# Rearranging the opening of a one-core encoder layer: two feature tiles first, and weight rests on GpSimd

## The reference

```python
x = _layernorm(x, ln_in_g, ln_in_b)
c_act = jax.nn.silu(c)
mod = (c_act @ w_ada[l] + b_ada[l]).reshape(B, N_SUBLAYERS, 3, D)
shift, scale, gate = mod[:, :, 0], mod[:, :, 1], mod[:, :, 2]

h = x * (1.0 + scale[:, 0, None, :]) + shift[:, 0, None, :]
y = _swiglu(h, ffn1_w_in[l], ffn1_w_out[l])
x = _layernorm(ALPHA * x + 0.5 * gate[:, 0, None, :] * y, post_ln_g[l, 0], post_ln_b[l, 0])
...
```

## Time and profile before

| | us |
|---|---|
| median of 3 timed runs | 955.99 (955.94 to 956.3) |
| the profiled execution: its time / its span | 956.35 / 954.6 |
| TensorE matmul busy | 938.6 (98% of the span) |
| VectorE busy | 506.7 (53%) |
| ScalarE busy | 375.0 (39%) |
| GpSimd busy | 267.3 (28%) |

### The profile page before, as it was taken

The page is one execution under the profiler, slowest core; times in us unless marked ns, Lnnn a source line. Parts: engine busy times, 40 slices in busy tenths (PEclk is TensorE's granted clock), DMA queues, the critical chain, the costliest instruction groups (busy, mean ns, idle before and its releaser), DMA issues.

```text
span 954.6 us, 10883 instructions
## 1 busy us (share of the span) xinstructions
PE 938.6 (98%) x4233; PEld 759.1 (80%) x4233; DVE 506.7 (53%) x713; ACT 375.0 (39%) x567; POOL 267.3 (28%) x222
## 2 busy tenths in 40 slices
PE   7999999999999999999999999999999999999997
PEld 5788888888888888788767687888888888888886
DVE  5956766545454865777666488632232222233334
ACT  6753223242222313564486556532322323221224
POOL 0021111111104512336843575611111111125125
PEclk9999999999999999999999999999999999999999
DMA  9836566556544663222521122232323222213302
GB/s 363 358 112 208 188 200 197 181 176 217 194 154 140 235 232 99 84 86 91 132 67 45 45 67 67 97 124 98 101 91 109 89 93 100 83 62 121 118 20 88
DMA packets 38499, 127.21 MB, mean 133 GB/s; under 512 B 4016, under 2 KB 6192, under 8 KB 38448
## 3 DMA queue, kind: packets, MB, share of 16 engines
q1 hardware_dynamic: 38448, 126.52, 39.4%
HBM read 123.36 MB, written 2.10 MB: 131 GB/s over the span
## 4 chain that ended last, share of the span: by engine, by line
PE 92%; DVE 3%; ACT 1%; POOL 1%; issue 1%; DMA 1%; SPq 0%; POOLq 0%; DVEq 0%; ACTq 0%
PE bank L601 28%; PE bank L603 28%; PE bank L602 28%; PE bank L957 1%; PE bank L981 1%; PE bank L680 1%; PE bank L686 1%; PE bank L687 1%; PE bank L968 1%; DMA x<-xT 1%; POOL cq L2014 0%; DVE w_lo L1081 0%; DVE lat L1534 0%; PE bank L727 0%; PE bank L874 0%
## 5 line engine op out<-in xcount | busy, mean ns | idle before, releaser
L1081 DVE TENSOR_TENSOR w_lo<-raw,w_hi 128x1024 fp32r<-128x1024 f32 x153 | 206.0, 1353 | 278.1 <-ACT w_hi L1053 277.7
L601 PE MATMUL bank<-h_hi,w_hi 128*128 128x512 f32 x727 | 284.5, 391 | 0.0
L603 PE MATMUL bank<-h_hi,w_lo 128*128 128x512 f32 x727 | 283.0, 389 | 0.0
L602 PE MATMUL bank<-h_lo,w_hi 128*128 128x512 f32 x727 | 282.9, 389 | 0.0
L1053 ACT ACTIVATE w_hi<-raw 128x1024 fp32r<-128x1024 f32 x153 | 155.9, 1031 | 189.2 <-PE bank L603 188.3
L1916 POOL TENSOR_TENSOR a_lo<-act_t,a_hi 128x512 fp32r<-128x512 f32 x44 | 58.9, 1339 | 422.0 <-ACT a_hi L1175 421.9
L601 PEld LDWEIGHTS bank<-h_hi,w_hi 128*128 128x128 f32 x727 | 136.6, 188 | 28.7 <-issue 0.5
L603 PEld LDWEIGHTS bank<-h_hi,w_lo 128*128 128x128 f32 x727 | 136.5, 188 | 28.5
L602 PEld LDWEIGHTS bank<-h_lo,w_hi 128*128 128x128 f32 x727 | 136.5, 188 | 27.8
L601 PE MATMUL bank<-a_hi,w_hi 128*128 128x512 f32 (+1 forms) x374 | 141.2, 377 | 0.0
L602 PE MATMUL bank<-a_lo,w_hi 128*128 128x512 f32 (+1 forms) x374 | 140.8, 377 | 0.0
(11 more groups left out here) (306 smaller groups left out, 1048.1 us busy)
## 6 DMA issues: line engine op xcount, KB each, us to landing
raw<-wunits SPq DMA_DIRECT2D x145, 512.0 KB, 3.2
ada_ring<-ada_w SPq DMA_DIRECT2D x56, 512.0 KB, 4.4
ada_first<-ada_w SPq DMA_DIRECT2D x16, 512.0 KB, 10.1
raw<-wunits SPq DMA_DIRECT2D x16, 384.0 KB, 2.9
x<-xT SPq DMA_DIRECT2D x4, 512.0 KB, 6.0
outT<-x SPq DMA_DIRECT2D x8, 256.0 KB, 2.6
K<-k_rope SPq DMA_DIRECT2D x2, 512.0 KB, 8.4
c_act<-c_rows SPq DMA_DIRECT2D x1, 512.0 KB, 7.9
```

The source lines that it names most:

```text
L601: mm(out, lh, rh, start=first, stop=False)
L602: mm(out, lh, rl, start=False, stop=False)
L603: return mm(out, ll, rh, start=False, stop=last)
L1081: nc.vector.tensor_tensor(lo, raw[:, slot, 0:width], hi.bitcast(F32), SUB).then_inc(s_lo, 1)
```

## The change

The x loads are eight instead of four, and unit 1 is loaded behind the first gate pair. ScalarE loads the table of Silu at the start, guesses the root ahead of rounding unit 0, normalises only the feature tiles 0 and 1 (256 columns of each token group) ahead of the first transposes, and rounds unit 1 ahead of h_hi[0] and unit 2 ahead of the affine tiles. GpSimd normalises tiles 2 and 3 and makes the rests of units 0 and 1. TensorE transposes tile 2 after tile 1's first matmuls. A few semaphores that nobody waited on go.

```diff
-X_LOADS = 4
+X_LOADS = 8
...
             unit(0)
+            ada_pair(0)
             unit(1)
-            ada_pair(0)
             ada_pair(1)
...
-                    if k + 2 < KD:
+                    if k == 1:
+                        pe.wait_ge(s_xnb, QB)
+                        transpose_x(2)
+                    if 1 <= k < KD - 2:
                         if k == 2:
                             pe.wait_ge(s_xna, 2 * QB)
                         transpose_x(k + 2)
...
+            preload(1, ACT.Silu)
             for t in range(QB):
                 act.wait_ge(s_bn, t + 1)
...
             preload(0, ACT.Abs_reciprocal_sqrt)
-            act_hi(act, 0)
             act.wait_ge(s_tv, 1)
             fn(trstd[:], tvar[:], ACT.Abs_reciprocal_sqrt).then_inc(s_tq, 1)
-            act_hi(act, 1)
-
-            def normal(t, i):
-                src = bank[TOKEN_BANK[i][t]][:] if i else x_tok[:, t, 0:TOK]
-                if i == 0:
-                    act.wait_ge(s_xk, t + 1)
-                fn(x_tok[:, t, i * TOK:(i + 1) * TOK], src, ACT.Identity,
+            act_hi(act, 0)
+
+            def normal_two(t):
+                act.wait_ge(s_xk, t + 1)
+                fn(x_tok[:, t, 0:2 * P], x_tok[:, t, 0:2 * P], ACT.Identity,
+                   scale=trstd[:, t:t + 1], bias=tshift[:, t:t + 1]).then_inc(s_xna, 1)
+
+            def normal_half(t):
+                fn(x_tok[:, t, TOK:2 * TOK], bank[TOKEN_BANK[1][t]][:], ACT.Identity,
                    scale=trstd[:, t:t + 1], bias=tshift[:, t:t + 1]).then_inc(s_xna, 1)
...
             for t in range(QB):
-                normal(t, 0)
+                normal_two(t)
+            act_hi(act, 1)
             act.wait_ge(s_tp, 1)
             act.wait_ge(s_full0, 2)
...
+            act_hi(act, 2)
             affine(0)
             affine(1)
-            act_hi(act, 2)
...
-                for n in range(2) if k == 0 else range(k + 1, min(k + 2, EARLY)):
+                if k == 1:
+                    dve.wait_ge(s_lo, 2)
+                for n in range(k + 1, min(k + 2, EARLY)) if k else ():
                     dve_lo(dve, n)
...
+            for n in range(2):
+                pool.wait_ge(s_hi, n + 1)
+                hi, lo = parts(n, 0, UNIT)
+                tt(lo, raw[:, n, :], hi.bitcast(F32), SUB).then_inc(s_lo, 1)
+            pool.wait_ge(s_tv, ROOT_STEPS)
+            for t in range(QB):
+                pool.wait_ge(s_xk, t + 1)
+                ts(x_tok[:, t, 2 * P:TOK], x_tok[:, t, 2 * P:TOK], trstd[:, t:t + 1], tshift[:, t:t + 1], MUL, ADD)\
+                    .then_inc(s_xnb, 1)
             ffn(0, 1, a_hi1, a_lo1)
```

More of the change, by code:

```diff
@@ L380, in build @@
         s_bn, s_tv = sem("x_stats"), sem("x_root")
-        s_xna = sem("x_normal")
+        s_xna, s_xnb = sem("x_normal"), sem("x_normal_by_pool")
         s_tok = sem("x_token_major")
@@ L394, in build @@
         s_nx = [None] + [sem(f"normal_steps{p}") for p in range(1, 4)]
-        s_hf = [sem(f"h_full{p}") for p in range(4)]
+        s_hf = [sem(f"h_full{p}") for p in range(3)]
         s_hh = [sem(f"h_hi_done{p}") for p in range(4)]
-        s_hl = [sem(f"h_lo_done{p}") for p in range(4)]
-        s_res = [sem(f"residual_scaled{p}") for p in range(4)]
+        s_hl = [sem(f"h_lo_done{p}") for p in range(3)]
+        s_res = [None] + [sem(f"residual_scaled{p}") for p in range(1, 3)]
         s_uh = [None] + [sem(f"plain_hi_done{p}") for p in range(1, 3)]
@@ L1275, in _ @@
                 if k < 3:
-                    normal(2 * k - 2, 1)
-                    normal(2 * k - 1, 1)
+                    normal_half(2 * k - 2)
+                    normal_half(2 * k - 1)
                 if k + 1 < KD:
```

## The result

| | before | after |
|---|---|---|
| median, compared on one chip | 956.07 us (7 runs) | 959.64 us (7 runs; 959.3 to 959.97) |
| the profiled execution: time / span | 956.35 / 954.6 | 959.3 / 957.5 |

The change makes the kernel slower by 0.36% (ratio 1.0036, 95% interval 1.0027 to 1.0045), 3.6 us between the medians and 2.9 us between the two profiled spans.

A forecast was written before the change was run, and what follows sets the result against it. TensorE is dense after the opening, so the start of tile 2's matmuls decides. The root gains 2.3 us, turns and moved transposes outweigh it, h_hi[2] comes 2.3 later: 955.99 + 2.3 = 958.3 us, range 955.0 to 959.6.

The forecast's parts named there:

- the main case: Opening: GpSimd's long subtractions hold VectorE in turns, and moved transposes delay tile 2; 958.3 us, span 957.1 to 959.2, chance 0.45.
- the third rival: Tiles 1 and 2: TensorE's clock stays low past 32 us, 1.2 us more, 959.5; chance 0.12.
- The root 2.3 us sooner: Opening: fewer transposes before the statistics, table load in idle time, guess ahead of rounding; root complete at 14.7, not 17.0.
- Two tiles first: ScalarE in the opening: four normals over 256 columns take 2.0 us, end 16.8; unit 1's rounding ends 17.8.
- VectorE and GpSimd take turns, tiny instructions too: Ahead of tile 0: VectorE's two-input instructions stand behind GpSimd's long subtractions; h_hi[0] starts at 22.0, 1.6 us later.
- Rival 1: Opening: GpSimd's work is hidden, full_col ready by 17.8; 954.1 to 955.3 us, likeliest 954.4; chance 0.16.
- rival 2: Opening: only wide VectorE instructions pay for turns; full_col ready at 19.5, h_hi[0] at 19.6; 957.6 us, chance 0.27.
- The multiply-adds: GpSimd's four 256-column normalisings: 0.53 us each alone; gate pair 1 still gives first_col[1] by 24.6 to 25.4.
- Transposes of tile 2 moved: Behind tile 1's four matmuls: affine(2) waits about 1 us extra, starts 29.6; h_hi[2] done at 32.8, +2.3.
- The sum: Whole kernel: h_hi[2]'s 2.3 us delay carried unshortened to the end; profiled run 958.65, median 958.3.
- Transfers change nothing: Loads of the opening: none added, later ones issued earlier behind a stream already full at 420 GB/s; no effect.

The follow-up runs named there:

- no_gpsimd: The changed kernel with GpSimd's rests and multiply-adds and the moved tile 2 transposes undone; early root, loads and ScalarE order stay: 954.5 us.
- rests_only: The kernel before, with only the rests of units 0 and 1 moved to GpSimd: 959.46 us.
- reading_beside: The kernel before plus four unused 512-column GpSimd additions on scratch from the root's end on: 961.26 us (one run).
- writing_beside: The kernel before plus ten 512-column GpSimd memsets, which only write scratch, from the root's end on: 956.0 us (one run).
- late_second_rest: The changed kernel, with GpSimd's second rest (unit 1) waiting for full_col: 960.42 us.
- transposes_only: The kernel before, with only tile 2's transposes moved behind tile 1's four matmuls: 957.44 us.
- scalar_normals_late: The changed kernel without its GpSimd work, ScalarE normalising all 512 columns; tile 2's transposes stay moved: 955.39 us.
- no_gpsimd_warm: The changed kernel without GpSimd work or moved transposes, with three instead of one extra matmuls ahead of tile 0's: 954.86 us.
- rests_on_vector: The changed kernel, with the rests of units 0 and 1 back on VectorE; GpSimd keeps the four multiply-adds: 956.6 us.
- kept_warm: The changed kernel with six instead of one idle matmuls between tile 0's transposes and h_hi[0]: 959.54 us.

## Why the prediction was right, and where its sizes were off

The forecast was 958.3 us, slower by 2.3; 959.64 was measured, slower by 3.6. That is at the upper edge of the whole range (959.6) and 0.4 above the 959.2 of the main case alone; the number lies nearer to the third rival's 959.5. That the main case is the right one is told by the trace, step by step, and not by the time.

- *The root 2.3 us sooner.* Right: 14.59 against 17.01 in the trace. The loads' share of it was 0.3 us and not 0.5 (the statistics end at 12.83 against 13.15). With the loads and the order on ScalarE, and without the rest of the change, it is worth 1.6 us of time (no_gpsimd).
- *Two tiles first.* 2.0 us for the four normals was 2.08. The narrowing bought nothing, since ScalarE then waited 4.4 us.
- *VectorE and GpSimd take turns, tiny instructions too.* Right, and close throughout: h_hi[0] at 21.98 (22.0), act_t[1] at 25.81 (25.8), h_hi[1] done at 27.29 (27.3). rests_only, reading_beside and writing_beside show the mechanism apart from the rest of the change. Rival 1 (GpSimd hides everything) and rival 2 (small ones slip in before a turn) fall with first_col's 2.17 us.
- *The multiply-adds.* The assumption "a multiply-add of 256 columns is 0.53" was wrong beside a busy VectorE: 7.85 us for four. The conclusion drawn from it, that they don't hold tile 1, held all the same (first_col[1] done at 24.52, predicted 24.6 to 25.4). That they might hold tile 2 the prediction never asked; in the changed kernel they tie with the matmuls, and in late_second_rest they do hold it.
- *Transposes of tile 2 moved.* The mis-sized step is "From 27.3 this gives 28.8 to 30.2; I take 29.6, with the clock recovering on the way at about 29 as before". affine(2) started at 30.37, just past the upper end. The four matmuls took 1.9 us, as taken; what was mis-sized is the time from the transposes' start to affine(2), for which 29.6 leaves 0.4 us and which measured 1.16 (29.21 to 30.37). About half of that excess goes with the clock, which did not recover (0.50 through the stretch at 30): in transposes_only, where it came back just as the transposes ran, the same piece took 0.76 (27.81 to 28.57). The other half was too short a term at either clock. That was rival 3's condition in a milder form: the clock was back at 31 and not past 32, tile 2's matmuls ran at full clock from 33.52 on, and only the transposes and the first matmul behind them were slow. This step's 0.8 us is more than all of what h_hi[2] missed (33.46 for 32.8). By itself the move was measured at +1.4 (transposes_only) and +0.9 (scalar_normals_late).
- *The sum.* +2.3 was +2.9 between the profiled executions, by the step above. The medians are 3.6 apart, since this profiled execution of before lay 0.3 above its median and that of the changed kernel 0.3 below; so I read 0.6 of the miss as scatter of single executions.
- *Transfers change nothing.* True of the changed kernel. It stops being true 2 us sooner: no_gpsimd and no_gpsimd_warm wait for unit 3, rests_on_vector 0.35 us for unit 2.

## What to carry to other kernels

Before work goes to GpSimd because it idles, list what VectorE does at that moment with two SBUF inputs. Where GpSimd subtracts or adds two SBUF tensors they take turns, and the price here was not a share of speed but up to a whole GpSimd instruction for each VectorE instruction on the chain, the two-column one as much as the wide one (2.2 us each). GpSimd's multiply-adds were the other way round, as the next section shows: they were late themselves. When a bundle of edits comes out slower, take the parts out one at a time and keep what pays: here the reordering alone was worth 1.6 us, and the offload, in the ladder's order, cost 4.2. A step moved to a later place should be priced at the slower clock if the engine ahead of it has been idle.

## What the hardware showed that I had not expected

- The turns are not even. A GpSimd subtraction of two tensors makes VectorE wait for its whole length: 2.25 us on a four-column product. A GpSimd multiply-add with two scalars for each partition, 256 columns wide, does the opposite: VectorE loses 0.15 to 0.24 us on four of its instructions (1.40 for 1.22, 0.39 for 0.16) and nothing on the others beside it, and GpSimd's instruction lasts 1.97 us on the mean (0.58 to 3.16), where one of that shape and form takes 0.59 elsewhere in the same trace. The groups of GpSimd's instructions in the changed kernel (busy us, mean ns, idle before):

```profile
L1965 POOL TENSOR_TENSOR w_lo<-raw,w_hi 128x1024 fp32r<-128x1024 f32 x2 | 6.6, 3321 | 11.2 <-ACT w_hi L1056 11.2
...
L1969 POOL TENSOR_SCALAR x_tok<-x_tok,trstd,tshift 128x256 f32<-128x256 f32 x4 | 7.8, 1973 | 0.0
...
L2054 POOL TENSOR_SCALAR x<-x,cols 128x256 f32<-128x256 f32 x4 | 2.3, 593 | 0.2
```

  Which part of such an instruction touches what VectorE holds, I did not test; that it stands still for some two VectorE instructions is only read from the overlap.
- A GpSimd subtraction of 128 x 1024 lasts 2.34 us with little beside it (rests_only) and 3.32 with VectorE's dot products.
- Extra matmuls ahead of tile 0 gained nothing measurable in either version. Six of them kept the clock up until 26.8 and it was low at tile 1 all the same (kept_warm); three held it through tiles 1 and 2, and in the execution traced the wait was then for a transfer (no_gpsimd_warm).
